# Ada sums on VectorE instead of GpSimd, rotary angles during feed-forward, inputs laid out on the host

## The reference, cut to what matters

```python
# first block: feed-forward, mixer, feed-forward in each of two layers
for layer in range(2):
    x = x + 0.5 * swiglu(rmsnorm(x, g[0]), ffn_w_in[layer, 0], ffn_w_out[layer, 0])   # 1024 -> 2 x 2816 -> 1024
    x = x + (even_mixer if layer == 0 else odd_mixer)(rmsnorm(x, g[1]), ...)
    x = x + 0.5 * swiglu(rmsnorm(x, g[2]), ffn_w_in[layer, 1], ffn_w_out[layer, 1])
x = rmsnorm(x, final_norm_g)
# second block
c_act = silu(c)                                         # c: 1 x 1024
for l in range(2):
    ada = c_act @ w_ada[l] + b_ada[l]                   # w_ada[l]: 1024 x 6144
    sh1, sc1, gt1, sh2, sc2, gt2 = split(ada, 6)
    y = mixer(x * (1 + sc1) + sh1, cos, sin, ...)       # cos, sin from positions
    x = layer_norm(DN_ALPHA * x + (1 + gt1) * y, ...)
    h = square(relu((x * (1 + sc2) + sh2) @ w_up[l])) @ w_down[l]     # 1024 -> 4096 -> 1024
    x = layer_norm(DN_ALPHA * x + (1 + gt2) * h, ...)
```

## Time and profile before

| | |
|---|---|
| median of 3 runs | 1989.61 us (1987.58 to 1997.01) |
| profiled execution, its own time | 1984.26 us |
| its span | 1982.5 us |
| busy: PE, DVE, ACT, POOL | 1840.3, 1406.2, 956.4, 829.4 us |
| mean granted clock | 0.959 |
| weights and Ada loaded | 345 MB, 175 GB/s |

### The profile page before, as it was taken

The page is one execution under the profiler, slowest core; times in us unless marked ns, Lnnn a source line. Parts: engine busy times, 40 slices in busy tenths (PEclk is TensorE's granted clock), DMA queues, the critical chain, the costliest instruction groups (busy, mean ns, idle before and its releaser), DMA issues.

```text
span 1982.5 us, 28192 instructions
## 1 busy us (share of the span) xinstructions
PE 1840.3 (93%) x11324; PEld 1624.9 (82%) x11324; DVE 1406.2 (71%) x1502; ACT 956.4 (48%) x1182; POOL 829.4 (42%) x392
## 2 busy tenths in 40 slices
PE   7999999999999999988899979988999899889997
PEld 6788798788888888867788869978888798878886
DVE  6987554499858995565988559856864489668643
ACT  5454453445434543445454342855543447555432
POOL 5967200097649766020976829900000069400000
PEclk9999997899999999999999978999999899999998
DMA  7777442366775876632587644334655344336550
GB/s 236 247 247 246 157 150 85 106 223 225 251 243 194 259 239 208 190 101 96 181 258 241 206 137 140 108 115 131 191 191 178 125 152 144 112 107 193 189 190 23
DMA packets 346549, 347.75 MB, mean 175 GB/s; under 512 B 15124, under 2 KB 341576, under 8 KB 346440
## 3 DMA queue, kind: packets, MB, share of 16 engines
q1 hardware_dynamic: 346408, 346.18, 53.9%
q10 hardware_dynamic: 32, 0.02, 0.0%
HBM read 345.11 MB, written 1.07 MB: 175 GB/s over the span
## 4 chain that ended last, share of the span: by engine, by line
PE 43%; issue 31%; POOL 12%; DVE 10%; ACT 3%; DMA 1%; POOLq 1%; SPq 0%; DVEq 0%; ACTq 0%
PE bank L861 19%; PE bank L860 10%; POOL arena L783 4%; POOL arena L749 4%; DVE wl L1734 3%; POOL arena L746 3%; PE bank L804 3%; PE bank L805 2%; PE bank L806 2%; DVE hx L1799 1%; PE bank L849 1%; ACT wh L1330 1%; DVE xn L1765 1%; PE bank L1228 1%; PE bank L1031 1%
## 5 line engine op out<-in xcount | busy, mean ns | idle before, releaser
L1734 DVE TENSOR_TENSOR wl<-raw,wh 128x2048 fp32r<-128x2048 f32 (+1 forms) x279 | 749.3, 2686 | 327.6 <-ACT wh L1330 327.3
L861 PE MATMUL bank<-xx,wh 128*128 128x512 f32 x1920 | 682.0, 399 | 0.0
L1330 ACT ACTIVATE wh<-raw 128x2048 fp32r<-128x2048 f32 (+1 forms) x279 | 525.9, 1885 | 251.6 <-PE bank L861 193.1
L860 PE MATMUL bank<-xx,wl 128*128 128x256 f32 x1920 | 544.8, 284 | 45.1 <-DVE arena L1790 22.0
L861 PEld LDWEIGHTS bank<-xx,wh 128*128 128x128 f32 x1920 | 365.3, 190 | 84.9
L861 PE MATMUL bank<-hx,wh 128*128 128x512 f32 x1216 | 427.7, 395 | 0.0
L860 PEld LDWEIGHTS bank<-xx,wl 128*128 128x128 f32 x1920 | 367.9, 192 | 53.4 <-issue 47.9
L746 POOL TENSOR_TENSOR arena<-arena,csil 128x2048 f32<-128x2048 f32 x48 | 223.1, 4647 | 394.7 <-DVE xx L1745 206.7
L804 PE MATMUL bank<-xx,wh 128*128 128x256 f32 x1136 | 333.4, 293 | 29.1 <-DVE xx L2084 15.3
L860 PE MATMUL bank<-hx,wl 128*128 128x256 f32 x1216 | 344.9, 284 | 0.0
L805 PE MATMUL bank<-xx,wh 128*128 128x256 f32 x1136 | 327.6, 288 | 0.0
(11 more groups left out here) (278 smaller groups left out, 1887.2 us busy)
## 6 DMA issues: line engine op xcount, KB each, us to landing
raw<-in_ffn_w_in SPq DMA_DIRECT2D x88, 1024.0 KB, 5.2
arena<-in_w_ada SPq DMA_DIRECT2D x48, 1024.0 KB, 7.8
raw<-in_w_in SPq DMA_DIRECT2D x36, 1024.0 KB, 4.9
raw<-in_ffn_w_out SPq DMA_DIRECT2D x32, 1024.0 KB, 5.7
raw<-in_w_up SPq DMA_DIRECT2D x32, 1024.0 KB, 5.4
raw<-in_w_down SPq DMA_DIRECT2D x32, 1024.0 KB, 5.1
raw<-in_ffn_w_out SPq DMA_DIRECT2D x16, 768.0 KB, 6.7
raw<-in_even_w_in SPq DMA_DIRECT2D x12, 1024.0 KB, 5.3
```

The source lines that it names most:

```text
L860: pe.matmul(o[:, 0:T], lo_w, halves[:, 0, :], start=start, stop=False, skip_group_check=True)
L861: return pe.matmul(o.rearrange("p (h t) -> p h t", h=2), hi_w, halves, start=False, stop=stop, skip_group_check=True)
L1330: act.activation(wh[:, c % RING, at], raw[:, c % RING, at], ACT.Copy).then_inc(hi_made.sem, 1)
L1734: dve.tensor_tensor(wl[:, c % RING, at], raw[:, c % RING, at], wh[:, c % RING, at].bitcast(F32), ALU.subtract).then_inc(lo_made.sem, 1)
```

## The change

It does six things.

1. Ada goes from GpSimd and TensorE to VectorE. The host lays `w_ada` out transposed, so that a block holds 256 outputs: output (j, p) has its 1024 weights in partition p. `csil` becomes the silu of c, 1024 values, in every partition. `ada_dots` makes two fused products with a sum over 1024 for a block; the sums are the outputs. `pool_ada` and `pe_ada` go.
2. `ada_dots` stands in VectorE's program at the end of steps 1, 2, 3, 5, 6, 8, 9 of the up phase (blocks 0 to 6) and behind `lo` in iterations 1, 3, 4, 6, 9 of the down phase (blocks 7 to 11). SyncE's issues of the blocks move too: in the down phase behind the loads of chunks 0, 1, 4, 6, 7. `dve_ada` stands in iteration 10, with `dve_fold` in ffn1 and ffn3.
3. The rotary angles: inputs loaded at the end of ffn1's program, GpSimd's part behind it, ScalarE's two sines in iteration 1 of ffn2's down phase. The tables lie where constants of even were.
4. The host lays out all weight chunks in the order of use, each chunk contiguous, 8 KB a partition (1 KB runs before). `w_uk`, `w_uv`, the small weights and the bias rows come ready; the last are scaled by 8 on ScalarE in odd.
5. `x` comes transposed in four DMAs, the vectors in one. `pe_setup` only waits for GpSimd's constants.
6. The result is stored transposed, eight DMAs straight from `x`, each when its tile is ready.

The core of the diff:

```diff
@@ sync: load and load_ada
+            if turn is None:
+                sp.dma_start(raw[:, c % RING, wide(c)], A["chunks"][c, :, wide(c)]).then_inc(loaded[c % RING].sem, 16)
+            else:
+                sp.dma_start(raw[:, c % RING, :], A["chunks"][bass.ds(source, 1), :, :]...).then_inc(loaded[c % RING].sem, 16)
...
                 if times is not None:
                     sp.wait_ge(ada_summed.sem, times)
+                sp.dma_start(ada_raw[:, slot, :], A["ada"][bass.ds(n + (24 * l + first), 1), :, :]...).then_inc(ada_loaded[slot].sem, 16)
...
                 if st == 1:
                     if s != "ffn0":
                         sp.wait_ge(x_ready.sem, x_ready.at(x_of[s]))
-                    for n in range(2):
-                        load_ada(n, n, ada_summed.at(s, 0) if s != "ffn0" else None)
+                    load_ada(0, 0, None)
+                if turn is not None and st == 2:
+                    load_ada(turn * 2 + 1, 1, shifted(ada_summed.at(s, 0), turn, 2))
+                if turn is not None and st == 4:
+                    load_ada(turn * 2 + 2, 0, shifted(ada_summed.at(s, 1), turn, 2))
+                if st in (8, 9):
+                    load_ada(st - 3, (st - 3) % 2, ada_summed.at(s, st - 4))
...
             for g, j, c, k, n in down_chunks(s):
-                load(c, w_out[:, k:k + n, g * 256:(g + 1) * 256], ("p (k n) -> p k n", {"k": n}))
-                if s in ADA_OF and j == 1:
-                    load_ada(8 + g, g % 2, ada_summed.at(s, 8 + g - 1))
+                load(c)
+                d = len(DOWN["ffn"]) * g + j
+                if s in ADA_OF and d in ADA_FETCH:
+                    n = ADA_FETCH[d]
+                    load_ada(n, n % 2, ada_summed.at(s, n - 1))
@@ the plan
+    ADA_AFTER = {1: 7, 3: 8, 4: 9, 6: 10, 9: 11}
+    ADA_FETCH = {0: 7, 1: 8, 4: 9, 6: 10, 7: 11}
@@ vector
+        def ada_dots(s, n, turn=None):
+            l, first = ADA_OF[s]
+            dve.wait_ge(ada_loaded[n % 2].sem, shifted(ada_landed(s, n), turn, 16))
+            for j in range(2):
+                w = ada_raw[:, n % 2, j * D:(j + 1) * D]
+                last = dve.tensor_tensor_reduce(w, w, csil[:, :], 1.0, 0.0, ALU.mult, ALU.add, dots[:, n % 2, j:j + 1])
+            last.then_inc(ada_summed.sem, 1)
+            dve.wait_ge(ada_summed.sem, shifted(ada_summed.at(s, n + 1), turn, 2))
+            ...
+            dve.tensor_tensor(adaT[:, l, 0, cols], dots[:, n % 2, :], vecT[:, 1, biases], ALU.add).then_inc(ada_biased.sem, 1)
@@ dve_ffn, up phase, end of a step
+                if st == 1:
+                    ada_dots(s, 0)
+                if turn is not None and st in (2, 3):
+                    ada_dots(s, st - 1, turn)
+                if st in (8, 9):
+                    ada_dots(s, st - 3)
@@ dve_ffn, down phase
                 if c < last:
                     lo(c + RING)
+                d = len(DOWN["ffn"]) * g + j
+                if KIND[s] == "ffn" and d in ADA_AFTER:
+                    ada_dots(s, ADA_AFTER[d])
+                if KIND[s] == "ffn" and d == 10:
+                    dve_ada(s)
+                    ...
@@ act_ffn, down phase
                 if c < last:
                     hi(c + RING)
+                if s == "ffn2" and (g, j) == (0, 1):
+                    act_rope()
@@ end of the program of sync
+        for k in range(KT):
+            sp.wait_ge(x_ready.sem, x_ready.at(xstage, k + 1))
+            sp.dma_start(out[:, k, :], x[:, k, :]).then_inc(stored.sem, 16)
```

More of the change, by code:

```diff
@@ L41 @@
 BIAS_COLS = 384
-ARENA = 20480
+ARENA = 19472
 ATT = 12 * 384
@@ L76, in constants, with tiles, laid_out @@
             turn[first + i, first + half + i] = 1.0
-    return {"buckets": buckets, "rope_freq": freq, "rope_turn": turn}
+    return bucket, {"rope_freq": freq, "rope_turn": turn}
+def tiles(w):
+    return w.reshape(-1, P, w.shape[-1]).transpose(1, 0, 2)
+def laid_out(inputs):
+    a = {n: np.asarray(v) for n, v in inputs.items()}
+    bucket, out = constants()
+    for n in ("gla_w_gate", "gla_b_gate", "fox_b_f", "positions_2", "c_2"):
+        out[n] = a[n]
+    out["chunks"], out["ada"] = weight_chunks(a), ada_chunks(a)
+    out["x"] = np.ascontiguousarray(tiles(a["x"][0].T))
+    vectors = np.zeros((P, 4, P), np.float32)
+    for n, row, at in VECTORS:
+        v = a[n].reshape(-1, P).T
+        vectors[:, at, row:row + v.shape[1]] = v
+    for l in range(2):
+        v = a["conv_dw_w_2"][l].reshape(-1, P).T
+        vectors[:, 2 + l, 0:v.shape[1]] = v
+    out["vectors"] = vectors
+    w = tiles(a["even_w_in"][0])
+    small = np.zeros((P, KT, 40), np.float32)
+    small[:, :, 0:16], small[:, :, 32:40] = w[:, :, 1536:1552], w[:, :, 3088:3096]
+    out["even_small"] = small
+    w = tiles(a["odd_w_in"][0])
+    out["odd_small"] = np.concatenate([w[:, :, 1792:1856], w[:, :, 1792:1856], w[:, :, 1856:1864]], 2)
+    out["w_uk"] = tiles(a["mla_w_uk"][0].reshape(D, LAT).T)
+    out["w_uv"] = tiles(a["mla_w_uv"][0].transpose(1, 0, 2).reshape(LAT, D))
+    out["bias_rows"] = a["t5_table"][bucket].T
+    return out
@@ L516, in build, with ada_landed @@
+    ADA_FETCH = {0: 7, 1: 8, 4: 9, 6: 10, 7: 11}
+    def ada_landed(s, n):
+        return 16 * (int(s[3:]) * ADA_PER_FFN // 2 + n // 2 + 1)
     block = ctx.enter_context(nc.Block())
-    N_IDENT, N_ONES, N_CONST = 2, 5, 18
+    N_IDENT, N_ONES, N_CONST = 2, 5, 17
     @block.sync
     def _(sp):
[L523 to L537, removed]
@@ L658, in _ @@
+        def sp_mix(s):
+            for n in range(26):
+                load(base[s] + n)
         for kind, s in STAGES:
@@ L1221, in pe_odd @@
             pe_out(s, c0 + 7)
-        def pe_ada(s):
-            pe.wait_ge(ada_summed.sem, ada_summed.at(s))
-            at = ADA_BANK[s]
-            for n in range(2 * ADA_PER_FFN):
-                last = pe.matmul(bank[at][:, T + n:T + n + 1], ada_sum[:, n // 2, (n % 2) * P:(n % 2 + 1) * P], ones[:, 0:1], start=True, stop=True)
-            last.then_inc(ada_turned.sem, 1)
         def pe_mix(s, moving):
@@ L2038, in mask @@
             def mask():
-                dve_ada("ffn2")
                 dve.wait_ge(mla_pe.sem, M_PE["K3"])
@@ L2158, in meanwhile @@
                 convolve(TAPS_PER_STEP)
-            if s == "mix0":
-                dve_ada("ffn3")
-                dve_fold(1)
             dve_attention(s, meanwhile)
@@ L2230, in _ @@
                 dve_rms(s)
-                if before == "ffn1":
-                    dve_ada(before)
-                if s == "rms5":
-                    dve_fold(0)
             if kind in ("ffn", "sq"):
@@ L2265 @@
     arrays, aps = {}, {}
-    for name, value in {**inputs, **constants()}.items():
+    for name, value in laid_out(inputs).items():
         a = _np.ascontiguousarray(value)
```

337 lines of the change are left out of this document (107 added, 230 removed).

## The result

The kernel after takes 1981.88 us (median of 11 runs, 1969.97 to 1985.34), the kernel before in the same runs 1990.78 (1978.44 to 1998.09). The ratio is 0.9945, with a 95% interval of 0.9927 to 0.9964: 0.55% faster, small, but the interval doesn't reach 1. The forecast was 1995.9. Its range (1923 to 2014) held the time, its sign did not: it had the change 0.3% slower.

The account below looks back on a forecast made before the run. The prediction took TensorE, busy for 93% of the span, to bound the kernel. 1984.26 - 68.1 saved + 74.3 lost gave 1990.5; with 5.35 from execution to median, 1995.9 us, range 1923 to 2014.

Parts of the forecast that it names:

- down phases: Four feed-forwards: weight loads queue in SyncE behind waits for VectorE's late Ada sums; 74.3 us lost, bounds 56 to 92.
- up phases: Four feed-forwards: without GpSimd beside it VectorE is fast again, TensorE's idle time goes; 24.2 us saved, bounds 15 and 26.
- start: Kernel start: first weight chunk issued behind five small loads instead of 17; some 4 us saved, bounds 2 and 6.
- even with its norm: Stage even: Ada's one-column matmuls go (5.4 us), with 1.6 for low clock around them; 7.0 us saved, bounds 5.4 and 12.
- rms3: Norm rms3: Ada's one-column matmuls go, TensorE then waits behind the statistics; 4.0 us saved.
- folds ahead of the last additions: ffn1 and ffn3: `dve_fold` and `dve_ada` at d10 stand ahead of the last additions; 1 us each lost.
- odd with its norms: Stage odd: Ada's matmuls and the key transposes before them go, less 0.6 for a copy they hid; 6.5 us saved.
- final norm, angles, modulation, mix0: TensorE's waits around the final norm's statistics shrink, 12.3 us saved; mix0 loses Ada's matmuls, 10.1 saved.
- chain of three links: Each down phase: waits for sums of blocks 7, 8, 9 delay d5, d7, d8; 16.4 us lost plus 1.8 for clock.
- B (the ring holds): Rival, down phases: loads behind the waits are not late enough to be seen; at best 1923 us; chance 0.28.
- C (the clock stays down): Rival, down phases: idle stretches keep TensorE's clock at half, 27 us more in four, 2022 us; chance 0.12.
- D: Rival, down phases: landings of 1.8 to 2.0 us fixed and 2.4 a MB, 10 us less for four, 1986; chance 0.10.

Follow-up runs that it names:

- second pair of executions: The kernel before and the kernel after, both unchanged, each profiled once more: 1986.03 us and 1975.15 us.
- free: Kernel after with only SyncE's fetches of Ada blocks 9, 10, 11 moved from behind the loads of d4, d6, d7 to behind d6, d8, d9: 1914.32 us.
- free_double: Against free, every pair of VectorE's Ada products with a sum made twice, 5.0 us a block instead of 2.5: 1938.88 us.
- after_again: The kernel after, unchanged, profiled once more: 1975.15 us, where its first profiled execution took 1983.43.

## Why the prediction was wrong by its sign, and where it was right

**The mechanism was right in both halves.** Savings and cost were placed where they occurred; the runs above try the down phases, the up phases and the angles, while the start, the end and the removal of Ada's matmuls are read from the traces alone. Worked out against the first pair of executions, in us:

| | predicted | measured |
|---|---|---|
| up phases | -24.2 | -23.5 (7.4, 7.8, 1.5, 6.7) |
| start | -4 | -4.3 |
| even with its norm | -7.0 | -8.9 |
| rms3 | -4.0 | -3.2 |
| folds ahead of the last additions | +2 | 0.8, inside rms3's row |
| odd with its norms | -6.5 | -4.1 |
| final norm, angles, modulation, mix0 | -12.3 - 10.1 | -21.7 |
| end | -2 | -2.3 |
| squared feed-forwards, mix1 | 0 | +1.0 |
| sum of the savings | -68.1 | -66.9 |
| down phases | +74.3 | +66.1 (16.3, 16.2, 17.1, 16.5) |

That single rows agree so closely is in part luck. Even gave 1.9 more and odd 2.4 less, which was not followed up. ffn2's up phase lost 2.9 us of idle time but won only 1.5, since its steps took 11.30 us instead of 11.09. In the second pair of executions the up phases differ by 29.1 us, beyond the bound of 26, and the down phases by 65.0. And mix0 came within 1.7 us of mix1, not 1.

**The step that was mis-sized is the chain of three links.** The prediction had 16.4 us of waiting and 1.8 of low clock a feed-forward. In ffn2 d1 ends on TensorE at 735.67 and d8 starts at 783.17, 47.5 later, against 32.2 before: 15.3 of waiting; 14.6 to 14.7 in the other three. From d8 to the end of the phase it takes 22.2 to 22.8 us where it took 20.7 to 20.9: 1.5 to 1.8 for the clock. The error is small in each link and comes three times. Behind `lo`, a block's products and their sum take 2.3 us (756.79 to 759.08), not 2.6: 0.9 a feed-forward. Block 10 and d7 land 7.2 to 7.5 us behind the issue, not 7.7, and the other two pairs 0.1 to 0.2 sooner than worked out: 0.6. The clock is 0.2 cheaper. That makes some 7 in four. In ffn2 the angles cost 0.7 instead of 1.5. Together that is nearly all of the difference. This term is the step that failed: 74.3 us where the traces have 66.1.

**The other half of the miss is the base.** 7.1 of the 14.0 us lie in the sum (1990.5 against the execution's 1983.43). The other 6.9 lie between execution and median: the execution of before was 6.5 below the median of its 11 runs, that of after 1.6 above its own. The forecast added 5.35 to both. Neither half alone makes the result: with 66.1 in place of 74.3 the forecast would have been 1987.7, only 0.1% below 1989.61. Two terms of 68 and 74 us with an uncertainty of a few each can't give the sign of their difference; the prediction knew that by its chances (0.35, 0.38, 0.27), and the one number that it put forward still had a sign.

**Rivals.** B (the ring holds) is the kernel free, not the kernel after: had the loads not been late, 1923 was the price, and free measured 1914.3. C (the clock stays down) didn't happen: a mean of 0.92 over 81 us is 13 us at half clock in a down phase, but most of it lies in groups that TensorE has to wait behind anyway (d7's eight tiles take 8.4 us, hidden in the wait for d8); 1.5 to 1.8 us are on the path. D had landings of 6.8 us for 2 MB and 1986: its direction was right (the time came out below the forecast), but its figure was too short, since the pairs of 2 MB took 7.2 us or more. The Trainium skill's fit ("DMA: Bandwidth & Descriptors", anatomy of one DMA, SWDGE path), 2.0 us and 436 GB/s, gives an estimate of 4.4 us for a lone MB. The trace has 4.8 with 8 KB rows and 5.3 with 1 KB rows, for loads issued by SyncE. The Trainium skill's table of specifications on the same page has rows of 512 B reach line rate; the trace doesn't agree: 0.5 us of a MB's landing hang on whether rows have 1 or 8 KB.

**What else held.** The fused product over 1024 took 1.22 us where 1.25 was taken from the nearest row; order and buffers of the up phase hid it whole, as free and the windows above show. What was too simple is the reason given for its safety: free_double shows that the slack was gone at twice the length, mostly at the ends of the down phases.

## What to carry to other kernels

When work moves from one engine to another, look at every queue whose waits now depend on it: here 66 of 67 us were given back because three fetches waited, ahead of weight loads, for something made late in the same loop, and one line that moves them behind later loads kept the whole gain. Write for each fetch which iteration makes what it waits for, and put it where the next load waits for that iteration anyway. Forecast the terms, and give the sign of a small difference of large terms only as a chance.

## What the runs showed of the hardware

In these traces GpSimd beside VectorE isn't a slowdown by a factor but an exclusion for whole instructions, seen only where VectorE reads both inputs from SBUF: the same phase lost 8 us with GpSimd's operations paced by their loads, and 56 with those operations back to back and VectorE's products added (180.8 against 124.6). The medians of a 1 MB landing differ by 0.5 us with the row length. A 2 MB pair lands in 7.2 or in 8.7 us, and it isn't its place that decides: block 7 with its chunk took 8.6 us in ffn2 of after and 7.2 there in after_again, the same kernel. TensorE's steps of 11.09 or 11.30 us at a full granted clock were not expected either. What decides was tried for neither.
